# A two-block network on one core: stick-breaking steps in another order, shares in two rounded parts, other banks for the up tiles, modulation rows on TensorE, and another order at the first border

## The reference, cut to what matters

```
mod = silu(c) @ w_ada + b_ada;  shift, scale, gate = split(mod, 3)          # c: (1, 1024), w_ada: (1024, 3072)
u = layer_norm(x) * (1 + scale) + shift                                     # x: (512, 1024)
proj = u @ w_in + b_in                                                      # 1024 x 12288
... pooled, short-conv and 31-tap-conv branches, merged by gates -> m
x = layer_norm(ALPHA * x + gate * (m @ w_out), ln_g, ln_b)                  # end of the first block
for l in 0, 1:
    h = rms_norm(x, norm_mix[l]);  dq, dk, dv, sq, sk, sv, g = split(h @ w_in[l])
    y_a = dilated_attention(dq, dk, dv) @ w_proj_a[l]      # 3 groups merged with shares s_g / sum s_g
    y_b = stick_breaking_attention(sq, sk, sv) @ w_proj_b[l]
    x = x + (sigmoid(g_a) * y_a + sigmoid(g_b) * y_b) @ w_out[l]
    h = rms_norm(x, norm_ffn[l])
    x = x + (silu(conv3(h @ w_up_a)) * (h @ w_up_b)) @ w_down[l]
out = rms_norm(x, norm_final)

# stick breaking, per head:  z = q k^T / 8;  A = exp(log_sigmoid(z) + sum of log_sigmoid(-z) over the keys between)
```

## Time and profile before

| | |
|---|---|
| time, median of 3 runs | 2242.89 us (2242.47 to 2247.31) |
| the profiled execution's own time | 2243.1 us |
| its span, first to last instruction | 2240.9 us |
| PE / PEld / DVE / ACT / POOL busy | 97% / 81% / 56% / 34% / 2% |
| mean granted TensorE clock | 0.987 |
| HBM read | 212.06 MB, 97 GB/s over the span |

### The profile page before, as it was taken

The page is one execution under the profiler, slowest core; times in us unless marked ns, Lnnn a source line. Parts: engine busy times, 40 slices in busy tenths (PEclk is TensorE's granted clock), DMA queues, the critical chain, the costliest instruction groups (busy, mean ns, idle before and its releaser), DMA issues.

```text
span 2240.9 us, 25627 instructions
## 1 busy us (share of the span) xinstructions
PE 2168.8 (97%) x10742; PEld 1805.2 (81%) x10742; DVE 1248.9 (56%) x1612; ACT 763.7 (34%) x1008; POOL 35.4 (2%) x46
## 2 busy tenths in 40 slices
PE   2999999999999799999999999999999999999998
PEld 2788888888888697977788888889797778888887
DVE  7798797953654836522755554234642375555422
ACT  1223232323343244344343333235434424333311
POOL 1000000000000110000000000000000000000000
PEclk7999999999999999999999999999999999999999
DMA  9323322332223122321223322322232222322231
GB/s 298 125 98 99 113 80 94 99 113 94 94 94 118 59 93 75 114 72 61 94 72 98 113 93 95 103 66 94 76 113 76 75 76 76 113 94 94 95 103 75
DMA packets 188239, 217.89 MB, mean 97 GB/s; under 512 B 3808, under 2 KB 167262, under 8 KB 188126
## 3 DMA queue, kind: packets, MB, share of 16 engines
q1 hardware_dynamic: 184128, 210.52, 28.6%
q10 hardware_dynamic: 3262, 3.60, 0.5%
q0 software_dynamic: 736, 2.15, 0.3%
HBM read 212.06 MB, written 4.19 MB: 97 GB/s over the span
## 4 chain that ended last, share of the span: by engine, by line
PE 89%; DVE 6%; ACT 2%; issue 2%; DMA 1%; POOL 0%; SPq 0%; POOLq 0%; ACTq 0%; DVEq 0%
PE psum L1604 28%; PE psum L1605 28%; PE psum L1606 28%; PE psum L1828 1%; DVE whl L468 1%; DVE adsum L1042 1%; PE psum L1861 1%; PE psum L1893 1%; PE psum L1873 1%; PE psum L1815 0%; PE psum L1844 0%; DMA x<-in_x 0%; DVE stat L1011 0%; PE psum L1920 0%; POOL stat L618 0%
## 5 line engine op out<-in xcount | busy, mean ns | idle before, releaser
L1604 PE MATMUL psum<-hT,whl 128*128 128x512 f32 (+1 forms) x2112 | 804.2, 381 | 8.5 <-DVE hT L1064 5.5
L1605 PE MATMUL psum<-hT,whl 128*128 128x512 f32 (+1 forms) x2112 | 796.9, 377 | 0.0
L1606 PE MATMUL psum<-hT,whl 128*128 128x512 f32 (+1 forms) x2112 | 796.8, 377 | 0.0
L468 DVE TENSOR_TENSOR whl<-raw,whl 128x1024 fp32r<-128x1024 f32 (+1 forms) x368 | 449.3, 1223 | 530.0 <-ACT whl L461 529.9
L461 ACT ACTIVATE whl<-raw 128x1024 fp32r<-128x1024 f32 (+1 forms) x368 | 384.5, 1048 | 481.5 <-PE psum L1606 441.2
L1604 PEld LDWEIGHTS psum<-hT,whl 128*128 128x128 f32 x2112 | 398.9, 189 | 91.4 <-DVE hT L1064 9.0
L1606 PEld LDWEIGHTS psum<-hT,whl 128*128 128x128 f32 x2112 | 399.1, 189 | 73.2
L1605 PEld LDWEIGHTS psum<-hT,whl 128*128 128x128 f32 x2112 | 399.3, 189 | 71.1 <-issue 0.5
L1604 PE MATMUL psum<-whl,ff 128*128 128x512 f32 x352 | 137.3, 390 | 2.2 <-DVE fsil L1583 2.2
L1606 PE MATMUL psum<-whl,ff 128*128 128x512 f32 x352 | 137.0, 389 | 0.0
L1605 PE MATMUL psum<-whl,ff 128*128 128x512 f32 x352 | 137.0, 389 | 0.0
(11 more groups left out here) (269 smaller groups left out, 2094.6 us busy)
## 6 DMA issues: line engine op xcount, KB each, us to landing
raw<-in_w_in SPq DMA_DIRECT2D x88, 1024.0 KB, 5.1
raw<-in_w_up SPq DMA_DIRECT2D x44, 1024.0 KB, 5.1
raw<-in_w_down SPq DMA_DIRECT2D x20, 1024.0 KB, 5.0
ada<-in_w_ada SPq DMA_DIRECT2D x12, 1024.0 KB, 11.0
raw<-in_w_branch SPq DMA_DIRECT2D x12, 1024.0 KB, 5.1
raw<-in_w_out SPq DMA_DIRECT2D x12, 1024.0 KB, 5.1
x<-in_x SPq DMA_DIRECT2D x4, 512.0 KB, 7.3
v_by_token<-vnat ACTq DMA_DIRECT2D x4, 512.0 KB, 2.9
```

Of the source, the lines that this page charges most:

```text
L468: nc.vector.tensor_tensor(whl_view(w, 1), raw_view(w), whl_view(w, 0).bitcast(F), ALU.subtract).then_inc(w_lo, 1)
L1604: M(out_, stat_hi, mov_hi, start=start, stop=False, **kw)
L1605: M(out_, stat_hi, mov_lo, start=False, stop=False, **kw)
L1606: return M(out_, stat_lo, mov_hi, start=False, stop=stop, **kw)
```

## The change: what it does, and the diff

1. **Start.** `c` gets a DMA of its own (`crow`, 8 x 128), first on SP's queue; PE transposes it and ACT takes `cact` from PSUM. SP no longer waits for the small vectors before the `w_ada` loads. Of the eight chunks of `w_ada`, four (0, 1, 5, 7) are multiplied on PE in row form: `cact` (one column) as the weights, 8 fp32 matmuls of 256 columns into one PSUM row each (`ada_product`); ACT copies the row out, PE turns it into columns (`ada_turned`). DVE keeps chunks 2 and 3 (one group) and 4 and 6 (256 columns each). In the modulation ACT writes the full value of the odd blocks as well, and DVE that of the even ones; the first weight splits are laid before and between. The first three tiles run together, staggered by one block (`together`).
2. **First border.** Other order of the steps on DVE, ACT, POOL and PE; DVE writes the low parts; POOL only takes roots.
3. **Stick breaking.** softplus at steps 0 and 1, high parts at 1 and 2, low parts at 2 and 3, both heads' exponents and exp at step 4, values at 5, output at 6.
4. **Shares.** Split into a rounded high part (ACT) and the rest (DVE); `share_wide` is 8 fp32r matmuls.
5. **Up tiles.** From the second pair on, the banks are moved on by 4.

```diff
+            sp.dma_start(crow[:], t["c"].rearrange("a b -> (a b)").rearrange("(r n) -> r n", n=P)).then_inc(s_c, 16)
-            sp.wait_ge(s_vec, 16 * vec_loads(False))
                 if q == 0:
-                    sp.wait_ge(s_adsum, 2)
+                    sp.wait_ge(s_mod, 1)
...
+            act.wait_ge(s_cT, 1)
+            A(cact, bank(7)[:, 496:504], ACT.Silu).then_inc(s_cact, 1)
+            for i_, q in enumerate(PE_CHUNKS):
+                act.wait_ge(arow_ps, i_ + 1)
+                A(adsum[0:1, q, :], bank(7)[32 * i_:32 * i_ + 1, P:P + 256], ACT.Copy).then_inc(arow_in, 1)
+            split_hi(0)
+            split_hi(1)
             act.wait_ge(s_modc, 1)
-            act.wait_ge(s_xT, 4)
             for ct in range(KT):
+                act.wait_ge(s_xT, 4 if ct == KT - 1 else 2)
+                if ct % 2:
+                    if ct > 1:
+                        act.wait_ge(h_lo, ct - 1)
+                    A(utmp[:, 1, :], bank(ct), ACT.Identity, bias=modc[:, ct:ct + 1], scale=modc[:, 8 + ct:9 + ct]).then_inc(u_act, 1)
                 A(hT[:, 0, ct, :], bank(ct), ACT.Identity, bias=modc[:, ct:ct + 1], scale=modc[:, 8 + ct:9 + ct]).then_inc(h_hi, 1)
+                if ct == 2:
+                    split_hi(2)
...
+            def ada_product(q):
+                r0 = 32 * PE_CHUNKS.index(q)
+                pe.wait_ge(s_ada[q], 16)
+                for k in range(KT):
+                    ins = M(bank(7)[r0:r0 + 1, P:P + 256], cact[:, k:k + 1], ada[:, q, k * 256:(k + 1) * 256], start=k == 0, stop=k == KT - 1)
+                ins.then_inc(arow_ps, 1)
...
+            together = PAIR_KEYS(0)[:3]
+            for k_ in range(KT + 2):
+                if k_ < KT:
+                    pe.wait_ge(h_lo, k_ + 1)
+                for i_, key in enumerate(together):
+                    k = k_ - i_
...
-                        if ph in (2, 3):
-                            sb_hi(2 * p + ph - 2)
-                        if ph in (4, 5):
-                            sb_exp(2 * p + ph - 4)
-                        if ph == 7:
+                        if ph in (1, 2):
+                            sb_hi(2 * p + ph - 1)
+                        if ph == 4:
+                            sb_exp(2 * p)
+                            sb_exp(2 * p + 1)
+                        if ph == 6:
                             sb_out(p)
...
+                act.wait_ge(share, l + 1)
+                A(shares[0:4, 0, :, :], mrow[0:4, 4:6, :], ACT.Copy).then_inc(share_hi, 1)
...
+                        dve.wait_ge(share_hi, l + 1)
+                        V.tensor_tensor(shares[0:4, 1, :, :], mrow[0:4, 4:6, :], shares[0:4, 0, :, :].bitcast(F), ALU.subtract).then_inc(share_lo, 1)
...
-                            ins = M(bank(2 + 2 * j + kind), sel[0:4, j, :], mrow[0:4, 4 + kind, :], start=True, stop=True)
+                            for part in range(2):
+                                ins = M(bank(2 + 2 * j + kind), sel_r[0:4, j, :], shares[0:4, part, kind, :], start=part == 0, stop=part == 1)
...
-            W_BANK[key] = (2 * key[2] + (key[0] == "up_b") * 2 - key[2] % 2) % 8
+            W_BANK[key] = (2 * key[2] + (key[0] == "up_b") * 2 - key[2] % 2 + (4 if key[2] > 1 else 0)) % 8
```

227 lines of the change are left out of this document (139 added, 88 removed).

## The result

| | before | after |
|---|---|---|
| time, median of 4 runs each, taken in turn on one chip | 2243.27 us (2242.47 to 2247.31) | 2209.52 us (2209.43 to 2209.58) |
| the profiled execution's own time | 2243.1 us | 2209.58 us |
| its span | 2240.9 us | 2207.1 us |

The ratio is 0.9846 [0.9829, 0.9863]: 33.8 us gained, where 22.4 were forecast. The forecast, 2220.5, is 11 us too high. The changed kernel was run twice more on another chip, at 2211.36 and 2210.72 us against 2245.49 and 2244.70 before: 34 us gained each time.

A forecast was written before the change was run, and what follows sets the result against it. PE, busy 97% of the span, bounds the kernel. Border 7.2, stick breaking 6.8, shares 6.0, up tiles 2.4 and start 0 sum to 22.4, taking 2242.9 to 2220.5 us; range 2209 to 2231.

The forecast's parts named there:

- I take the half level for the products: Start: row products on PE run at the half clock level, 6.9 us each instead of 3.5, except chunk 5's.
- the start's term: Start: 0 us gained, later coefficients eating what three tiles side by side give; bounds 3.4 lost and 9.4 gained.
- The rival with the products at the full level: Start: products run at the full clock level, giving up to 9.4 us more, total 2211; chance 0.18.
- its bound of 43.6: Start: modulation coefficients come at 43.6 us if all four products run at the full level, 9.4 us gained.
- Shares: Shares, both layers: faster fp32r matmuls and less half-level clock behind them gain 6.0 us, the middle between 7.6 and 4.2.
- the case in which a half-level stretch stays: Shares: 3.4 us at the half clock level remain behind the matmuls in each layer; gain 4.2 us.
- Stick breaking: Stick breaking: waits on softplus low parts (2.7) and ahead of the second pair's scores (4.1) go; gain 6.8 us.
- First border: First border: first tiles start 9.8 us earlier, DVE's chain then decides the second half; gain 7.2 us.
- Its lower bound of 4: First border: the gain is at least 4 us, if the splits stretch as before, twice 2.1.
- Up tiles: Up tiles: two 1.1 us waits ahead of the row product with `w_down` go; gain 2.4 us, bounds 1 and 2.6.
- late small vectors: Start, rival: small vectors arrive only behind the big loads, near 43 us, making the kernel slower, 2245; chance 0.04.
- new wait in the shares: Shares, part of the next-wait rival: a new ACT-DVE round trip cuts their gain to 2; total 2231, chance 0.16.

The follow-up runs named there:

- h_triple: Changed kernel with each of the eight rounded share matmuls done three times (24 instead of 8): 2224.39 us, ratio 0.9915.
- s_dve: Changed kernel with all eight chunks of `w_ada` multiplied on DVE again: 2213.12 us, ratio 0.9853.
- s_apart: Changed kernel with its first three tiles one after another again instead of staggered together: 2213.91 us, ratio 0.9858.
- b_pool: Changed kernel with the low parts of token blocks 0 and 1 at the first border written by POOL again: 2216.16 us, ratio 0.9876.
- u_banks: Changed kernel with the up tiles in the banks they had before: 2214.38 us, ratio 0.9865.
- s_best: Changed kernel with reordered start on TensorE and ACT, repeated matmuls before the fourth product, fewer repeated transposes than s_keep before the first tile: 2208.40 us, ratio 0.9837.
- h_fp32: Changed kernel with the shares spread by four plain fp32 matmuls (8 in the trace) again: 2217.23 us, ratio 0.9883.
- s_keep: Changed kernel with rows turned before product 5, half of product 5 repeated, two weight splits before last row copy, transposes repeated up to first tile: 2211.34 us.

## Why the prediction was off, step by step

**The step that failed: "I take the half level for the products".** It made the start's term 0. The argument ran from the 4-row matmuls of the shares, behind which the clock had fallen, to the one-column products, "narrow too". The runs show the opposite for products: the clock rose within the first one, and the second and third ran at the full level in eight of the nine executions. The forecast had them end at 30.5, 38.8 and 49.9; they ended at 27.4, 35.3 and 44.0, and the coefficients came at 46.5 instead of 53.0. Of these 6.5 us, 3.1 are the second product, 1.6 the fourth, 0.9 the sums between, 0.6 the steps behind the last product and the rest the transposes, which ran at the full level too but then waited 1.1 for their chunk. So the half level taken for the products is 4.7 of the 6.5. What followed the coefficients was forecast right: 21.3 us to the end of the three tiles, 21.3 measured. The last 0.9 is the kernel before, whose three tiles end at 75.2 and not at 74.3. The rival with the products at the full level (2211, chance 0.18) was the case that came, with the coefficients at 46.5 instead of its bound of 43.6, as the fourth product was half slow. The Trainium skill ("TensorE: Matmul & The Clock Gate", Part 1) has sustained activity release the clock; the products agree with it. The 4-row matmuls of h_triple, without idle time, do not.

The step hides a second misreading. The start gained little by the products as such (s_dve: 1.2 us) and most by the rest: 3.0 by the staggered tiles, and 3.2 between the kernel before and s_apart (27.5 us from coefficients to the third tile's end, and 24.3). These 3.2 are a difference and were not taken apart: ACT's share of the modulation and the splits laid ahead are in them, and about 1 us of the clock, as the half level covers 5.4 us of the tiles before (53.6 to 59.0) and 3.6 in s_apart.

**Shares: mis-sized, 7.9 instead of 6.0.** The sum of all its parts was 7.6, and I took the middle to the case in which a half-level stretch stays. The matmuls took 2.1 us, not 1.8; the low part cost nothing, where 1.0 was set aside. The stretch behind them is a matter of chance: a quarter of 28 cases. The 4.2 us of the other case was thus a real possibility, but the middle was too low: with a quarter of the places slow, at 1.6 us each, the mean is 7.1. The profile after showed the better case, and that much of it is luck.

**Stick breaking: 8.0 instead of 6.8.** Both waits went, as forecast. The 6.8 are the idle time alone; the matmuls beside the waits lose more: over the first layer's stretch the 264 tile matmuls took 64.5 us from start to start before, 3.4 of it idle, and 60.6 after, which is 0.5 us a layer besides the idle time.

**First border: 7.8 instead of 7.2.** Near in the sum, by steps that err both ways: first tiles 9.8 us earlier than in the earlier trace rows, less what the start gave; measured 787.9 - 7.4 - 770.2 = 10.3. Second half at 795.3, which is 787.9 with the start's 7.4 taken off; measured 787.3. Fourth tile read at 806.8, or 799.4; measured 799.1. PE's wait of 3.9 us between the halves came as 1.3 and 0.8 us idle, 1.1 at the half level and some 0.7 of longer work. The splits took 1.22 us. The prediction read the 4.50 us of two splits as both stretched; only the second was, from 1.22 to 3.36, and b_pool shows why. Its lower bound of 4 doesn't follow either: twice 2.1 off 7.2 leaves 3.0.

**Up tiles: 2.4, measured 2.45.** u_banks gives the same in reverse.

**The rivals.** No late small vectors: they were transposed at 22.95. No new wait in the shares; at the border PE waits 4.7 + 1.3 + 0.8 us on DVE's chain, which is where the forecast's own steps had it wait.

## What to carry to other kernels

A wait of TensorE is worth more than its length: it may be followed by 3.4 us or twice that at the half level, how long it is changes between executions of the same program (3.4 and 6.8 us at the border of the changed kernel), and so a term that rests on the clock is best given as two cases with a chance, not as their middle. When a chain is shortened, look at what TensorE does in the time won: here over half of the 1.0 and 2.0 us first won at the start came back as slow matmuls. Repeated work prevented that in one profiled execution of s_best, and its median shows no gain from it. And before a narrow shape is taken as slow by analogy with another narrow shape, the spacing of the first of them in any trace should be read; 4 rows by 512 columns and 128 rows by one weight column behaved in opposite ways.

## What was not expected of the hardware

- Eight fp32 matmuls with one weight column and 256 moving columns (16 in the trace) take 3.61 us at the full level and 6.54 mostly at the half level (h_fp32). The clock rose within the first such product, and the second ran at the full level, in all 14 profiled kernels that have them.
- In a run of 24 rounded matmuls with 4 rows, without idle time, the clock fell to the half level after 5.3 and 4.4 us, for 6.8 us, in both layers; eight of them, 2.1 us, are followed by 3.4 us of it in 7 of 28 cases.
- Beside a POOL step that reads SBUF, DVE steps with two SBUF inputs took 2.24 and 3.37 us instead of 1.28 and 1.23 and ended 1.1 us behind POOL's; one that reads PSUM kept its 1.22.
- Where a 2 us wait stands ahead of narrow scores, the clock fell in both layers of one kernel and in none of the kernel before. What decides it in an execution stays open.
- 14 transposes behind small sums, without idle time, ran at the half level for 3.4 us (s_keep), where 28 behind a product ran at the full level (the changed kernel).
